# Down projections of five FFNs: one part of the k tiles as seven half products

## The reference

```python
def swiglu(x, w_in, w_out):
    g, u = jnp.split(x @ w_in, 2, axis=-1)
    return (jax.nn.silu(g) * u) @ w_out

h = h + 0.5 * swiglu(rms_norm(h, ffn1_norm[i]), ffn1_w_in[i], ffn1_w_out[i])
x = x + swiglu_2(rmsnorm(x, norm_ffn[l]), w_gate_up[l], w_down[l])
```

## Time and profile before

| | us |
|---|---|
| median of 3 runs | 2758.37 |
| lowest and highest | 2755.64, 2758.88 |
| the profiled execution | 2757.22 |
| its span in the trace | 2755.4 |
| PE busy | 2732.0 (99%) |
| DVE busy | 1684.5 (61%) |
| ACT busy | 1353.1 (49%) |
| POOL busy | 1597.1 (58%) |

### The profile page before, as it was taken

One profiled execution on the slowest core, in us unless ns is written; L12 is line 12 of the kernel. 1 busy time (PEld: TensorE's weight loads), 2 busy tenths in 40 slices (PEclk: granted clock), 3 DMA queues, 4 the chain that ended last, 5 costly groups with the idle time before them and its releaser, 6 DMA issues.

```text
span 2755.4 us, 46269 instructions
## 1 busy us (share of the span) xinstructions
PE 2732.0 (99%) x16664; PEld 2348.6 (85%) x16664; DVE 1684.5 (61%) x2823; ACT 1353.1 (49%) x2136; POOL 1597.1 (58%) x892
## 2 busy tenths in 40 slices
PE   9999999999999999999999999999999999999999
PEld 7998877899889998888999886665688888799987
DVE  6778147677716775135777416589788464467740
ACT  5555257555525554243555433566444444455541
POOL 5776445677547776444777443158633373377763
PEclk9999999999999999999999999999999999999999
DMA  3224322222332233332223332111222342123332
GB/s 139 107 107 118 105 84 83 94 107 107 115 98 92 107 115 111 100 110 85 92 107 124 111 104 69 54 54 62 84 77 77 100 153 77 54 93 111 117 106 78
DMA packets 80679, 267.82 MB, mean 97 GB/s; under 512 B 11168, under 2 KB 13216, under 8 KB 80560
## 3 DMA queue, kind: packets, MB, share of 16 engines
q1 hardware_dynamic: 77904, 262.01, 28.2%
q10 hardware_dynamic: 2656, 4.26, 0.5%
HBM read 263.09 MB, written 2.10 MB: 96 GB/s over the span
## 4 chain that ended last, share of the span: by engine, by line
PE 93%; DVE 4%; ACT 2%; issue 1%; DMA 0%; POOL 0%; ACTq 0%; SPq 0%; DVEq 0%
PE bank L481 17%; PE bank L482 16%; PE bank L483 16%; PE bank L742 11%; PE bank L743 11%; PE bank L744 11%; PE bank L570 1%; PE bank L568 1%; PE bank L569 1%; PE bank L2095 1%; PE bank L2963 1%; PE bank L2695 0%; PE bank L2104 0%; PE bank L2675 0%; PE bank L1277 0%
## 5 line engine op out<-in xcount | busy, mean ns | idle before, releaser
L476 POOL TENSOR_TENSOR ring_lo<-w_stage,ring_hi 128x1024 fp32r<-128x1024 f32 (+2 forms) x196 | 464.1, 2378 | 526.4 <-ACT ring_hi L444 486.6
L469 POOL TENSOR_TENSOR ring_lo<-w_stage,ring_hi 128x1024 fp32r<-128x1024 f32 x108 | 267.2, 2481 | 383.7 <-ACT ring_hi L444 383.7
L444 ACT ACTIVATE ring_hi<-w_stage 128x1024 fp32r<-128x1024 f32 (+2 forms) x304 | 305.7, 1017 | 338.9 <-PE bank L483 292.6
L842 POOL TENSOR_TENSOR ring_lo<-w_stage,ring_hi 128x1024 fp32r<-128x1024 f32 x196 | 363.5, 1855 | 164.8 <-ACT ring_hi L948 164.5
L482 PE MATMUL bank<-h_lo,ring_hi 128*128 128x512 f32 x880 | 342.4, 389 | 0.0
L481 PE MATMUL bank<-h_hi,ring_hi 128*128 128x512 f32 x880 | 342.4, 389 | 0.0
L483 PE MATMUL bank<-h_hi,ring_lo 128*128 128x512 f32 x880 | 342.3, 389 | 0.0
L481 PE MATMUL bank<-xg_hi,ring_hi 128*128 128x512 f32 x816 | 333.6, 409 | 4.7 <-DVE h_raw L1107 3.6
L742 PE MATMUL bank<-xsum,s_w 128*128 128x256 f32 x1176 | 324.9, 276 | 0.0
L744 PE MATMUL bank<-xsum,s_w 128*128 128x256 f32 x1176 | 324.8, 276 | 0.0
L743 PE MATMUL bank<-xsum,s_w 128*128 128x256 f32 x1176 | 324.8, 276 | 0.0
(11 more groups left out here) (533 smaller groups left out, 6723.4 us busy)
## 6 DMA issues: line engine op xcount, KB each, us to landing
w_stage<-w_up SPq DMA_DIRECT2D x220, 512.0 KB, 3.9
w_stage<-w_down SPq DMA_DIRECT2D x80, 512.0 KB, 3.6
w_stage<-merge SPq DMA_DIRECT2D x36, 512.0 KB, 3.2
w_stage<-w_down SPq DMA_DIRECT2D x40, 384.0 KB, 3.1
w_stage<-hg_qfg SPq DMA_DIRECT2D x12, 512.0 KB, 3.3
w_stage<-rec_r SPq DMA_DIRECT2D x8, 512.0 KB, 3.2
w_stage<-rec_y SPq DMA_DIRECT2D x8, 512.0 KB, 3.2
w_stage<-rec_out SPq DMA_DIRECT2D x8, 512.0 KB, 3.2
```

Of the source, the lines that this page charges most:

```text
L444: act.activation(w_hi[:, r, 0:w], w_stage[:, r, 0:w], ACT.Copy).then_inc(w_hi_ready, 1)
L469: pool.tensor_tensor(w_lo[:, r, 0:w], w_stage[:, r, 0:w], f32(w_hi[:, r, 0:w]), ALU.subtract).then_inc(w_lo_ready, 1)
L476: pool.tensor_tensor(w_lo[:, r, 0:w], w_stage[:, r, 0:w], f32(w_hi[:, r, 0:w]), ALU.subtract).then_inc(w_lo_ready, 1)
L842: pool.tensor_tensor(wb_lo[:, r, cs], w_stage[:, r, cs], f32(wb_hi[:, r, cs]), ALU.subtract).then_inc(w_lo_ready, 1)
```

## The change

In the output pairs 2-3, 4-5 and 6-7, the 8 k tiles of one part (k 4 to 7 and 18 to 21) are made as seven half products of 4 k tiles by 256 columns: `M1`, `more` into the left half of out0 and of out1, `M5`, `M7`, `M6`, and `more` into the right half of out0. The parts are now 8, 8 and 6 k tiles with the block in the middle; the first pair stays as it was, but takes the block's part last, so that its units 2 and 3 are 768 columns wide and 4 and 5 are 1024.

- Four sums of h over its two row halves (`hsum`, each 128 x 1024) are made by VectorE between its low 13 and low 14. ScalarE makes their high halves (`sum_high`), GpSimd their low ones (`sum_low`). They lie over `xg_hi` and `xg_lo`, so the norm's high and low halves of outputs 0 to 5 move behind the last block.
- Per pair four sums of weights are made (`w_sums`, `w_lows`, the rows and `s3` on GpSimd), and six adds put the products together (`out_sums`).
- M7's weights (`s3_down`) lie in four tiles of h that are no longer read by then.
- Slots of the ring are 4608 bytes apart in place of 4096, so that the slots that lie 64 bytes aside (`wb_hi`, `wb_lo`) don't overlap the next; a wait for that in the up stage goes.

```diff
+PITCH = UNIT + P
...
-DOWN_UNITS = ((0, 0), (1, 0), (0, 1), (1, 1), (0, 2), (1, 2), (2, 0), (2, 1), (2, 2), (3, 0), (3, 1), (3, 2))
-DOWN_K = (12, 13, 14, 15, 0, 1, 2, 3, 16, 17, 8, 9, 10, 11, 4, 5, 6, 7, 18, 19, 20, 21)
+DOWN_PARTS = ((12, 13, 14, 15, 0, 1, 2, 3), (4, 5, 6, 7, 18, 19, 20, 21), (16, 17, 8, 9, 10, 11))
+BLOCK_PART = 1
+PART_TURNS = ((0, 2, 1), (0, 1, 2), (0, 1, 2), (2, 1, 0))
+DOWN_UNITS = tuple((2 * j + m, part) for j in range(KD // 2) for part in PART_TURNS[j] for m in range(2))
+DOWN_ROWS = sum(DOWN_PARTS, ())
+DOWN_K = sum((DOWN_PARTS[part] for part in PART_TURNS[0]), ())
...
+    s1_down = place("s1_down", [P, 2, T], F32R)
+    u_add_down = place("u_add_down", [P, T])
+    sum2 = place("sum2", [P, T])
+    s2_down = place("s2_down", [P, 2, T], F32R, at=under_ubuf - 256 + 4 * ASIDE)
+    hsum = place("hsum", [P, 4, 2, 4, HALF], F32R, at=under_xg)
+    hsum_f = place("hsum_f", [P, 4, 2, 4, HALF], at=under_xg)
 
...
+        def m7_down():
+            hi, lo = s3_down(h_hi)
+            xh, xl = h_sum(2)
+            for k in range(4):
+                wh, wl = (t[:, k // 2, P * (k % 2):P * (k % 2) + P] for t in (hi, lo))
+                pe.matmul(M7_OUT, wh, xh[:, k, :], start=k == 0, stop=False)
+                pe.matmul(M7_OUT, wh, xl[:, k, :], start=False, stop=False)
+                mm = pe.matmul(M7_OUT, wl, xh[:, k, :], start=False, stop=k == 3)
+            return mm
...
+        def down_block(j):
+            n, u = down_pair(j), down_unit(j, BLOCK_PART, 0)
+            out0, out1 = bank[2 * j % 4], bank[2 * j % 4 + 1]
+            p = u % RING // 2
+            pe.wait_ge(w_lo_ready, L.base + u + 1)
+            pe.wait_ge(block_add, pair_count(i, n, 5, -1))
+            product(M1_OUT, w_block(p, 0, 0), h_block(X00)).then_inc(block_mm, 1)
+            more(left(out0), w_block(p, 0, 1), h_block(X10)).then_inc(unit_used, 1)
+            pe.wait_ge(w_lo_ready, L.base + u + 2)
+            pe.wait_ge(pool_lo_ready, after_hsum_lo(i, 1))
+            more(left(out1), w_block(p, 1, 1), h_sum(3))
+            pe.wait_ge(wsum_lo_ready, after_wsum_lo(i, "S1", n))
+            pe.wait_ge(block_copied, pair_count(i, n, 1, 1))
+            product(M5_OUT, (s1_down[:, 0], s1_down[:, 1]), h_sum(0)).then_inc(block_mm, 1)
+            pe.wait_ge(pool_lo_ready, after_s3_lo(i, n))
+            m7_down().then_inc(block_mm, 1)
+            pe.wait_ge(wsum_lo_ready, after_wsum_lo(i, "S2", n))
+            product(M6_OUT, (s2_down[:, 0], s2_down[:, 1]), h_sum(1)).then_inc(block_mm, 1)
+            more(right(out0), w_block(p, 1, 0), h_block(X11)).then_inc(unit_used, 1)
+
+        def down_pair_products(j):
+            pe.wait_ge(taken, L.rbase + 2 * j + 2 - RING)
+            for at, part in enumerate(PART_TURNS[j]):
+                if part == BLOCK_PART:
+                    down_block(j)
+                    continue
+                for m in range(2):
+                    u = down_unit(j, part, m)
+                    pe.wait_ge(w_lo_ready, L.base + u + 1)
+                    last = len(DOWN_PARTS[part]) - 1
+                    for c, k in enumerate(DOWN_PARTS[part]):
+                        mm = three_passes(pe, bank[(2 * j + m) % 4][:], u % RING, c, h_hi[:, k, :], h_lo[:, k, :],
+                                          at == 0 and c == 0, at == 2 and c == last)
+                    mm.then_inc(unit_used, 1)
+
+        down_first_pair()
+        for j in range(1, KD // 2):
+            down_pair_products(j)
 
...
+        def sum_low(t):
+            pool.wait_ge(wsum_hi_ready, after_hsum_hi(i, t))
+            if t < 2:
+                pool.wait_ge(xsum_done, after_hsum(i, 1 + 2 * t))
+            pool.tensor_tensor(hsum[:, t, 1], hsum_f[:, t, 1], f32(hsum[:, t, 0]), ALU.subtract).then_inc(pool_lo_ready, 1)
+
+        def row(u, c):
+            r, cs = u % RING, slice(c * T, 2 * T)
+            pool.wait_ge(w_hi_ready, L.base + u + 1)
+            pool.tensor_tensor(wb_lo[:, r, cs], w_stage[:, r, cs], f32(wb_hi[:, r, cs]), ALU.subtract).then_inc(w_lo_ready, 1)
+
+        def pair(j):
+            n, u = down_pair(j), down_unit(j, BLOCK_PART, 0)
+            r = u % RING
+            hi, lo = s3_down(h_hi)
+            row(u, 0)
+            pool.wait_ge(w21_copied, pair_count(i, n, 1, 1))
+            pool.tensor_tensor(w21_stage(r), w_stage[:, r, 0:T], w21_stage(r), ALU.subtract).then_inc(s3_done, 1)
+            row(u + 1, 1)
+            pool.wait_ge(wsum_hi_ready, after_wsum_hi(i, "S3", n))
+            pool.tensor_tensor(lo, in_halves(w21_stage(r)), f32(hi), ALU.subtract).then_inc(pool_lo_ready, 1)
+
+        for u in range(6):
+            plain(u)
+        sum_low(0)
+        sum_low(3)
+        plain(6)
+        plain(7)
+        sum_low(2)
+        sum_low(1)
+        for j in range(1, KD // 2):
+            u = down_unit(j, BLOCK_PART, 0)
+            pair(j)
+            for v in range(u + 2, min(u + 6, L.n)):
+                plain(v)
 
     def act_x11(act, i, gain):
...
-        for k in range(7, KF):
+        for k in range(7, 14):
             low(k)
...
-        return i
+        dve.wait_ge(unit_used, U.base + U.n)
+        dve.wait_ge(taken, U.rbase + 2 * KF)
+        hs = [hsum_f[:, t, 1] for t in range(4)]
+        (k0, c0), (_, c1), (k1, _) = X00, X01, X10
+        h00, h01, h10, h11 = h_raw[:, k0, c0], h_raw[:, k0, c1], h_raw[:, k1, c0], h_raw[:, k1, c1]
+        dve.tensor_tensor(hs[0], h01, h00, ALU.subtract).then_inc(xsum_done, 1)
+        dve.wait_ge(xsum_done, after_hsum(i, 0))
+        dve.tensor_tensor(hs[1], h11, hs[0], ALU.subtract).then_inc(xsum_done, 1)
+        dve.tensor_tensor(hs[2], h11, h01, ALU.subtract).then_inc(xsum_done, 1)
+        dve.wait_ge(xsum_done, after_hsum(i, 1))
+        dve.tensor_tensor(hs[3], h10, hs[1], ALU.subtract).then_inc(xsum_done, 1)
+        dve.wait_ge(xsum_done, after_hsum(i, 3))
+        for k in range(14, KF):
+            low(k)
...
+        def sum_high(t):
+            act.wait_ge(xsum_done, after_hsum(i, t))
+            act.activation(hsum[:, t, 0], hsum_f[:, t, 1], ACT.Copy).then_inc(wsum_hi_ready, 1)
...
+        sum_high(0)
+        plain(4)
+        plain(5)
+        sum_high(3)
+        sum_high(2)
+        sum_high(1)
+        plain(6)
+        plain(7)
+        for j in range(1, KD // 2):
+            n, u = down_pair(j), down_unit(j, BLOCK_PART, 0)
+            copy21(n, u)
+            s1_high(n)
+            row(u, 0)
+            squares(2 * j - 2)
+            row(u + 1, 1)
+            s4_high(n, u)
+            s3_high(n, u)
+            squares(2 * j - 1)
+            s2_high(n)
+            plain(u + 2)
+            plain(u + 3)
+            copy_m1(n)
+            plain(u + 4)
+            plain(u + 5)
+        act.wait_ge(unit_used, L.base + down_unit(KD // 2 - 1, BLOCK_PART, 1) + 1)
+        for m in range(KD):
+            if m == KD - 2:
+                plain(L.n + 2)
+            if m >= KD - 2:
+                act.wait_ge(taken, L.rbase + m + 1)
+            tile_high(m)
+            if m >= KD - 2:
+                squares(m)
+
...
+        def w_sums(j):
+            n, r = down_pair(j), down_unit(j, BLOCK_PART, 0) % RING
+            u = down_unit(j, BLOCK_PART, 0)
+            w11, w12, w22 = w_stage[:, r, 0:T], w_stage[:, r, T:2 * T], w_stage[:, r + 1, T:2 * T]
+            dve.wait_ge(w21_copied, pair_count(i, n, 1, 1))
+            dve.tensor_tensor(S12_BANK[:], S12_BANK[:], w22, ALU.add).then_inc(wsum_done, 1)
+            dve.wait_ge(wsum_hi_ready, after_wsum_hi(i, "S1", n))
+            dve.tensor_tensor(s1_down[:, 1], S12_BANK[:], f32(s1_down[:, 0]), ALU.subtract).then_inc(wsum_lo_ready, 1)
+            dve.wait_ge(w_loaded[r], 16 * (L.base // RING + u // RING + 1))
+            dve.tensor_tensor(S12_BANK[:], S12_BANK[:], w11, ALU.subtract).then_inc(wsum_done, 1)
+            dve.wait_ge(wsum_done, after_wsum(i, "S2", n))
+            dve.tensor_tensor(S4_BANK[:], w12, S12_BANK[:], ALU.subtract).then_inc(wsum_done, 1)
+
+        def w_lows(j):
+            n, r = down_pair(j), down_unit(j, BLOCK_PART, 0) % RING
+            dve.wait_ge(wsum_hi_ready, after_wsum_hi(i, "S4", n))
+            dve.tensor_tensor(wb_lo[:, r + 1, 0:T], S4_BANK[:], f32(wb_hi[:, r + 1, 0:T]), ALU.subtract).then_inc(wsum_lo_ready, 1)
+            dve.wait_ge(wsum_hi_ready, after_wsum_hi(i, "S2", n))
+            dve.tensor_tensor(s2_down[:, 1], S12_BANK[:], f32(s2_down[:, 0]), ALU.subtract).then_inc(wsum_lo_ready, 1)
+
+        def out_sums(j):
+            n, (ua, ga) = down_pair(j), (u_add_down, g_add_down)
+            dve.wait_ge(block_copied, pair_count(i, n, 1, 1))
+            dve.wait_ge(block_mm, after_block(i, "M6", n))
+            dve.tensor_tensor(right(ua), M6_OUT, left(ua), ALU.add).then_inc(block_add, 1)
+            dve.wait_ge(block_add, after_add(i, "U2", n))
+            dve.tensor_tensor(left(ga), M7_OUT, right(ua), ALU.add).then_inc(block_add, 1)
```

(28 more changed lines are left out.)

285 lines of the change are left out of this document (184 added, 101 removed).

## The result

| | before | after |
|---|---|---|
| median, us | 2757.26 | 2790.48 (4 runs, 2790.28 to 2792.89) |
| ratio | | 1.0123 [1.0111, 1.0135] |
| profiled execution, us | 2757.22 | 2790.28 |
| span in the trace, us | 2755.4 | 2788.5 |

The kernel became 1.2% slower. Forecast was 2771 with 2748 to 2786, so the direction was right and the time lies outside the range, at the rival "they alternate everywhere" (2791).

The account below looks back on a forecast made before the run. TensorE was taken to bound the kernel, busy 2732.0 of 2755.4 us. Terms: −20.4 saving, +1.2 for M7, +27.1 waits, +5.1 clock, sum +13.0, giving 2771 us against the median; range 2748 to 2786.

Parts of the forecast that it names:

- they alternate everywhere: Rival: GpSimd and VectorE take turns, 10.5 us late in four down projections, 8.5 in down3; 2791 us, chance 0.07.
- The lows in a streak never let it in: VectorE's back-to-back lows shut GpSimd out until they end; waits of 1.9 us each in down0, down2 and down4.
- waits and clock: All TensorE waits in the down projections, 27.1 us, plus 5.1 for the lower granted clock after them.
- the 6.45 of unit 4: Unit 4's low half on GpSimd, 1.84 us undisturbed, took 6.45 beside back-to-back lows; read as the streak shutting GpSimd out.
- between two kinds of instruction: Boundary where GpSimd was said to get in, as before the cross attention (9.79 us); argued against the longer-streaks rival, chance 0.18.
- the saving: TensorE in the five down projections: half products save 20.4 us, less 1.2 for M7's slower passes.
- M7's 120 ns: M7's weights lie in h, not 64 bytes aside, so its passes take 120 ns each; +1.2 us in all.
- TensorE's busy time: Sign that the forecast is right: it falls by 19 us plus what the clock takes.
- down3: ScalarE waits for the final gain before unit 4's high half, so unit 5 comes 8.5 us late, without an engine collision.
- down1: Unit 4's low half is issued into the streak and held to its end; 5.0 us at unit 5, 5.6 with unit 6.
- down0's chain: Second pair of down0: GpSimd delays VectorE's softplus and S5 angles, so the block of pair 1 waits 7.3 us.
- The clock: TensorE's granted clock drops after each of three waits over 3 us, 1.7 us lost each time; +5.1 us.

Follow-up runs that it names:

- e1: The changed kernel, but GpSimd holds its four sum lows and units 6 and 7 until the lows of h are done; 2775.4 us.
- e3: The kernel before, with parts of 8, 6 and 8 k tiles and nothing else, so that units 4 and 5 are 1024 wide; 2762.7 us.
- e10: The kernel before, with VectorE waiting for its own low 13 before low 14 in each down projection; 2757.51 us in one run.
- e5: The changed kernel, but GpSimd waits for low 17 before unit 4; 2783.95 us in one run.
- e13: e9 with ScalarE's and VectorE's queues reordered, mainly pair 1's block inputs and copy of M1 ahead of squares and residuals, and two TensorE waits split; 2749.74 us.
- e2: e1, with ScalarE's wait for the final gain moved from ahead of down3's units to the first norm tile that needs it; 2773.68 us.
- e9: The changed kernel with sum lows on VectorE, GpSimd's units 6 and 7 after all lows, the final gain's wait late, the fourth sum behind lows 14 to 17; 2758.36 us.
- e6: e2, with GpSimd waiting for pair 1's S1 sums before units 6 and 7, and unit 8's row between its sum lows; 2779.67 us.
- e7: e6, with TensorE waiting for its own last pass ahead of each block; 2782.95 us.

## Why the prediction was wrong

**The step that failed: "The lows in a streak never let it in".** From it followed that GpSimd would be shut out from low 14 on, with 1.9 of waits in down0, down2 and down4. They have 8.9 each, because the two engines take turns. Up to there the forecast had held: the fourth sum ends 17.3 us after the first pass, as forecast, and low 14 is waited for by 1.18 where 1.3 was forecast. Then GpSimd was not shut out. The forecast for waits and clock was 32.2; the downs are longer than the 116.68 that they take unhindered by 9.9, 6.7, 9.8, 10.0 and 9.8, together 46.2. The rival priced this at 10.5 for each of four downs, which is near for three and 3.8 too much for down1, where TensorE waits for two lows only. Its 2791 has two errors that cancel: waits and clock of 52.2 are 6.0 too many, and the saving of 19.2 is 5.2 too much. e1 shows the mechanism directly: take GpSimd's work away from the lows, and they take 7.00 in place of 20.11. What I made of the 6.45 of unit 4 was half true: e3 has it again, and e10 and e5 show that it needs a long unbroken run of VectorE behind it. In the changed kernel the four sums break the run, and from there GpSimd always had the next instruction queued. The row that I gave too little weight was the earlier trace rows, where the same two kinds of instruction alternated for 9.79 us. I took it for boundaries "between two kinds of instruction"; its four m_lo are all of one kind. The Trainium skill, page "SBUF — State Buffer", section "Who interferes with whom", says that the shared port pair is an exclusive lock and that the order of issue, not the shape of the operation, decides who blocks. The traces agree where GpSimd's next instruction was queued (2.8 us a turn in down0 of the changed kernel), and not where a request was held over seven lows (6.45 us).

**A term mis-sized: the saving.** It was taken as 20.4 − 1.2 = 19.2. Unhindered downs are 116.68 against 119.48, 2.8 each, 14.0 in all. A block of 84 passes takes 9.92 us, 118 ns a pass, where I had taken 113 ns from the end of the up stage. TensorE of the changed kernel, first pass of a block (pair 2 of down0) and first pass behind it:

```profile
313.12 0.28 PE L797 MATMUL bank<-h_hi,ring_hi 128*128 128x256 f32 x1
323.04 0.40 PE L498 MATMUL bank<-h_hi,ring_hi 128*128 128x512 f32 x1
```

The trace of before had both paces: in an up stage 72 such passes take 8.48 us (117.8 ns) and the next 72 take 8.17 (113.5).

```profile
62.91 0.28 PE L742 MATMUL bank<-xg_hi,ring_hi 128*128 128x256 f32 x1
...
71.39 0.28 PE L742 MATMUL bank<-xg_hi,ring_hi 128*128 128x256 f32 x1
...
79.56 0.28 PE L742 MATMUL bank<-xsum,s_w 128*128 128x256 f32 x1
```

I had read the last 33 passes of a stage, the end of a long run of them; a block is the beginning of one. With 14.0 the forecast of 2771 would have been 2776. M7's 120 ns was right. TensorE's busy time, which was to fall by 19, fell by 4.1, and by 11.5 in e13; why that is less than the 14.0 by the starts of the passes isn't shown.

**down3: right.** 8.5 of wait and 1.7 of clock were forecast, 10.0 came, 6.78 and 1.09 of waits and some 2.1 of passes at the lower granted clock (0.97 over the stretch). The gain comes at 1561.17, 21.2 after the first pass, as forecast. e2 shows that the final gain was the cause, and e3 that part of it comes from the wider units alone.

**down1: the place right, the mechanism not.** 5.6 at unit 5 was forecast, with unit 4's low half held until the lows end; it is asked for at 737.80, in the second low of the run, and gets in at the next boundary. 1.76 stands at unit 5, and five smaller waits behind it make 6.0. That the total comes near 5.6 is luck.

**down0's chain: right in mechanism, absent in the result.** The wait of 7.3 shows up where the lows aren't held (6.5 in e1, 5.9 at the next row in e9). The changed kernel had paid the same time already at the lows. I had added two waits that exclude each other.

**The clock.** 5.1 was charged for three waits over 3 us; there was one, in down3. A threshold of 3 us was my choice; in e3 waits of 1.08 and 1.52 us in down3 were followed by passes at the lower clock as well, 1.4 in all, while the 8.9 us of down0 in the changed kernel, in seven waits of at most 1.3, left the granted clock at 1.00.

**The chances.** Alternation had 0.07. The range left it out on purpose and ended at 2786. It rested on one observation of a held GpSimd instruction against one of alternation, and the evidence did not bear odds of six to one.

## What to carry to other kernels

Before new work is put on GpSimd beside VectorE's two-operand instructions, count how many of its instructions will be queued there, and charge each VectorE instruction on the path the full length of one of them; where that is too much, let GpSimd wait for the last instruction that TensorE needs, or move the work to VectorE. A stage that shortens TensorE by a few us has its price in the queues around it: name for every product each input and what stands ahead of it in the queue of its maker, the smallest copy too. Take a pace from rows that begin as the new stretch will begin, behind the same kind of pass.

## What the runs showed of the hardware

- An unbroken run of VectorE instructions of 0.6 us on two tiles of SBUF held a GpSimd one off for several us (6.45 and 5.77 in place of 1.8 and 2.4), in the kernel before and in e3. There the request came in the ninth instruction of the run or later. Within the first six behind a wait of VectorE it got in at the next boundary (2.36 in e10, 2.76 in e5). From then on they took turns, 2.8 us a turn with 1024-wide GpSimd instructions. What exactly makes a run hold stays open.
- VectorE instructions of 0.17 us on 8 columns are held as long as large ones (2.41 and 2.32 in e9).
- Passes of 256 columns went at 118 ns behind 512-column ones and at 113 later, in an up stage. The last 24 of a block of e6, behind waits of 1.9 and 3.3 in that block (down1), went at 113 too. e7 shows that a drain ahead of the block doesn't change it; the cause stays open.
